# Recurrence prepared within the value projection, head norms in sixteen rows, and more unread products, in a two-block transformer kernel

## The reference

```python
def rwkv_features(h, ...):
    kk = heads(k * k_k)
    kk = kk * lax.rsqrt(jnp.maximum(jnp.sum(kk * kk, axis=-1, keepdims=True), 1e-24))   # norm of each head
    ...
    decay = jnp.exp(-jnp.exp(-jax.nn.softplus(-w_raw) - 0.5))
    a = jax.nn.sigmoid(heads(a0[d] + (xa @ a1[d]) @ a2[d]))

def wkv_scan(...):        # first over the context, then over x, forward and backward
    S = (S * w_t[:, :, None, :]
         - jnp.einsum('bhij,bhj->bhi', S, kk_t)[..., None] * kka_t[:, :, None, :]
         + v_t[..., None] * k_t[:, :, None, :])
    y = jnp.einsum('bhij,bhj->bhi', S, r_t)

def rwkv_readout(y, r, k_sum, v, g, r_k, ln_g, ln_b, wo, dtype):
    mean = jnp.mean(y, axis=-1, keepdims=True)
    var = jnp.mean(jnp.square(y - mean), axis=-1, keepdims=True)
    yn = ((y - mean) * lax.rsqrt(var + GN_EPS)).reshape(B, L, D_MODEL) * ln_g + ln_b
    bonus = (jnp.sum(r * k_sum * r_k, axis=-1, keepdims=True) * v).reshape(B, L, D_MODEL)
    return ((yn + bonus) * g) @ wo

def context_attention(q, k, v):
    p = jax.nn.softmax(q k^T * NA_HEAD_DIM ** -0.5)
    return p v
```

## Time and profile before

| | us |
|---|---|
| median of 3 runs | 2656.08 |
| lowest, highest | 2654.51, 2663.36 |
| profiled execution | 2654.95 |
| its span | 2653.2 |
| granted clock, mean over the span | 0.937 |

### The profile page before, as it was taken

One profiled execution on the slowest core, in us unless ns is written; L12 is line 12 of the kernel. 1 busy time (PEld: TensorE's weight loads), 2 busy tenths in 40 slices (PEclk: granted clock), 3 DMA queues, 4 the chain that ended last, 5 costly groups with the idle time before them and its releaser, 6 DMA issues.

```text
span 2653.2 us, 46388 instructions
## 1 busy us (share of the span) xinstructions
PE 2372.0 (89%) x19956; PEld 1958.6 (74%) x19956; DVE 1750.3 (66%) x3332; ACT 1021.3 (38%) x1892; POOL 67.0 (3%) x70
## 2 busy tenths in 40 slices
PE   6899978999989978889887889997989999997998
PEld 5775457787766567778886789996677879666886
DVE  6966788766745476767766578665355865754577
ACT  2134242322321223543332354344245654543465
POOL 0300000000000000000000000020000011000000
PEclk9897989999999989999999899997779999997999
DMA  7420426556522100000001377730045853002475
GB/s 299 145 109 1 173 100 250 211 209 230 213 113 81 47 0 3 3 3 3 3 11 66 145 269 290 267 144 32 1 159 214 334 191 138 12 1 96 180 296 205
DMA packets 47278, 347.99 MB, mean 131 GB/s; under 512 B 5248, under 2 KB 5248, under 8 KB 5728
## 3 DMA queue, kind: packets, MB, share of 16 engines
q1 hardware_dynamic: 45936, 334.52, 33.7%
q0 software_dynamic: 1136, 10.50, 1.0%
HBM read 343.95 MB, written 1.05 MB: 130 GB/s over the span
## 4 chain that ended last, share of the span: by engine, by line
PE 73%; DVE 20%; ACT 4%; issue 2%; DMA 1%; DVEq 0%; ACTq 0%; POOLq 0%
PE banks L533 23%; PE banks L927 8%; PE banks L1775 5%; DVE arena L612 3%; PE banks L1022 3%; PE banks L2520 3%; PE banks L2521 3%; PE banks L2522 3%; PE banks L1001 3%; PE banks L782 2%; PE banks L1652 2%; PE banks L1846 2%; PE banks L2551 1%; PE banks L2553 1%; PE banks L2552 1%
## 5 line engine op out<-in xcount | busy, mean ns | idle before, releaser
L612 DVE SCALAR_TENSOR_TENSOR arena<-weight_slots,silu_c,arena 128x256 f32<-128x256 f32 x776 | 328.3, 495 | 0.0
L514 DVE TENSOR_TENSOR moe_w_low<-weight_slots,moe_w_high 128x2048 fp32r<-128x2048 f32 x96 | 218.0, 2289 | 71.9 <-ACT moe_w_high L505 71.0
L927 PE MATMUL banks<-arena,weight_slots 128*128 128x256 f32 (+1 forms) x768 | 231.8, 460 | 19.0 <-DVE arena L1567 11.7
L927 PEld LDWEIGHTS banks<-arena,weight_slots 128*128 128x128 f32 x768 | 149.3, 196 | 95.4 <-issue 73.9
L505 ACT ACTIVATE moe_w_high<-weight_slots 128x2048 fp32r<-128x2048 f32 x96 | 181.3, 1911 | 24.7 <-PE banks L2553 19.8
L505 ACT ACTIVATE mlp_w_high<-weight_slots 128x2048 fp32r<-128x2048 f32 x64 | 122.2, 1910 | 170.6 <-PE banks L533 124.6
L1775 PE MATMUL banks<-weight_slots,arena 64*64 64x64 f32 (+1 forms) x3648 | 150.8, 225 | 36.8 <-DVE weight_slots L2088 15.5
L514 DVE TENSOR_TENSOR mlp_w_low<-weight_slots,mlp_w_high 128x2048 fp32r<-128x2048 f32 x64 | 146.3, 2286 | 48.5 <-ACT mlp_w_high L505 48.4
L1775 PEld LDWEIGHTS banks<-weight_slots,arena 64*64 64x64 f32 x3648 | 141.6, 136 | 44.9 <-issue 16.3
L2520 PE MATMUL banks<-moe_w_high,slots_x 128*128 128x512 f32 x320 | 133.5, 417 | 11.8 <-DVE moe_w_low L514 11.8
L1927 ACT ACTIVATE weight_slots<-banks 128x512 f32<-128x512 f32 x80 | 47.8, 597 | 230.1 <-DVE weight_slots L2088 201.7
(11 more groups left out here) (384 smaller groups left out, 5119.9 us busy)
## 6 DMA issues: line engine op xcount, KB each, us to landing
weight_slots<-weights SPq DMA_DIRECT2D x318, 1024.0 KB, 4.8
arena<-small POOLq DMA_DIRECT2D x1, 2560.0 KB, 9.0
arena<-x_t POOLq DMA_DIRECT2D x1, 2048.0 KB, 16.6
arena<-bias POOLq DMA_DIRECT2D x1, 2048.0 KB, 9.5
constants<-consts POOLq DMA_DIRECT2D x1, 1395.0 KB, 21.1
out_t<-arena SPq DMA_DIRECT2D x1, 1024.0 KB, 3.9
parameters<-params POOLq DMA_DIRECT2D x1, 775.0 KB, 9.9
arena<-pool_inv POOLq DMA_DIRECT2D x1, 512.0 KB, 10.4
```

What stands on the lines that cost most here:

```text
L514: nc.vector.tensor_tensor(self.pair(j)[1], slot(j, 0, SLOT), self.pair(j)[0], ALU.subtract).then_inc(*v.step("used", j))
L612: nc.vector.scalar_tensor_tensor(a_, w, c, a_, ALU.mult, ALU.add).then_inc(*v.step())
L927: ins = nc.tensor.matmul(psum(b, 0, w), slot(j, k, 256, i * P, P), moving(k), start=(k == 0), stop=(k == KT - 1))
```

## The change

1. **Head norm of the removal keys.** The eight sums go by accumulation into one tile of 16 rows (a row per head, new constant heads), behind wv block 0. One maximum, root and reciprocal of 16x512 replace eight of each. A constant SPREAD of 16x1024 (a copy) is the stationary operand of eight products that bring the 16 rows back to 128 behind wv block 1; the removal-key instruction reads them from PSUM.
2. **Chunk 0 of the recurrence** is prepared within the value projection. wkv_tensor and wkv_vector get parts: raws(0) behind block 1, orders(0) and raws(1) before the last half block; VectorE's part 0 behind its copies of block 1, part 1 behind those of block 2. ScalarE's sigmoids and decays of chunk 0 stand after its copies of block 1.
3. **Steady chunks.** raws(c+2) stand behind orders(c+1) at a chunk's end, no longer at level 1. raw_in(c+1) follows the masks. running(c+1,0) is at level 1, running(c+1,1) at level 2 ahead of turned, and ScalarE's sigmoids(c+1) stand ahead of inverse_out at level 1.
4. **Readout.** The variance of the eight tiles is accumulated into 16 rows, with one root, one reciprocal of 16x256, and eight spreading products; the bonus products have a loop of their own ahead.
5. **Unread products.** Context, causal and differential attention are filled too, context's into bank 6. The fill is 512 columns wide in the first 8 steps and 256 in the later ones, in sparse attention too (8 wide, 27 narrow).
6. **Router.** One unread product of 512 columns ahead of the counts and three behind them.

The diff, cut to its core:

```diff
-        def fill():
-            nc.tensor.matmul(psum(7), cn("ones"), cn("ident", 0, 512), start=True, stop=True)
+        def fill(u, b):
+            w = 512 if u < RAISE else 256
+            nc.tensor.matmul(psum(b, 0, w), cn("ones"), cn("ident", 0, w), start=True, stop=True)
...
         class ContextAttention(LatentAttention):
             name = "context_attention"
+            filled = True
+            fill_bank = 6
...
-            def kk_sum(t):
-                b = take_bank(pe, ("kk_sum", t))
-                pe.wait_ge(*after("kk_squares", t))
-                nc.tensor.matmul(psum(b), cn("block_ones"), root_of(t), start=True, stop=True).then_inc(*pe.step("kk_sum", t))
+            def kk_sums():
+                b = take_bank(pe, ("kk_sum",), [6])
+                for t in range(KT):
+                    pe.wait_ge(*after("kk_squares", t))
+                    ins = nc.tensor.matmul(psum(b, 0, 512, slice(0, 16)), head_rows(t), root_of(t), start=(t == 0),
+                                           stop=(t == KT - 1))
+                ins.then_inc(*pe.step("kk_sum"))
+
+            def kk_spread(tiles):
+                for t in tiles:
+                    b = take_bank(pe, ("kk_spread", t), range(6))
+                    pe.wait_ge(*after("kk_inverse"))
+                    nc.tensor.matmul(psum(b), head_columns(t), HEAD_ROOT, start=True, stop=True).then_inc(
+                        *pe.step("kk_spread", t))
...
                 for seg in range(2):
-                    b = take_bank(pe, ("wv", jj, seg))
+                    if (jj, seg) == (3, 1):
+                        wkv_tensor(pe, 1)
+                        pe.stage("project_wv")
+                    b = take_bank(pe, ("wv", jj, seg), range(6))
...
                 if jj == 0:
+                    pe.stage("removal_key")
+                    kk_sums()
                     low_rank("g", "g1", 1, [X])
-                    pe.stage("project_wv")
+                elif jj == 1:
+                    pe.stage("removal_key")
+                    kk_spread(range(KT))
+                    wkv_tensor(pe, 0)
...
-            raws(0)
-            for d in range(2):
-                orders("bm", 0, d, WK["B"][:, d], "beta")
-            for d in range(2):
-                orders("gm", 0, d, WK["G"][:, d], "gamma")
+            if part == 0:
+                raws(0)
+                return
+            if part == 1:
+                for d in range(2):
+                    orders("bm", 0, d, WK["B"][:, d], "beta")
+                for d in range(2):
+                    orders("gm", 0, d, WK["G"][:, d], "gamma")
+                raws(1)
+                return
...
                     if lv == 1:
                         seed(c, 0)
                         seed(c, 1)
-                        if c < 7:
-                            raws(c + 1)
...
+                if c < 6:
+                    raws(c + 2)
...
-                    if ahead and lv == 3:
+                    if ahead and lv == 2:
                         running(c + 1, 1)
...
                     if ahead and lv == 1:
-                        raw_in(c + 1)
-                    if ahead and lv == 2:
                         running(c + 1, 0)
...
-                v.wait_ge(*after("taken", "y_var", t))
-                nc.vector.reciprocal(RD[:, t], RD[:, t]).then_inc(*v.step())
-                v.wait_ge(*v.own)
-                stt(YC[:, t], YC[:, t], pr("lng", t, 1), RD[:, t], ALU.mult, ALU.mult).then_inc(*v.step())
+            spread_vector(v)
+            v.wait_ge(*after("taken", "y_var"))
+            nc.vector.reciprocal(RD[0:16, 0], RD[0:16, 0]).then_inc(*v.step("y_inverse"))
+            for t in range(KT):
+                v.wait_ge(*after("y_spread", t))
+                stt(YC[:, t], YC[:, t], pr("lng", t, 1), psum(bank_of(("y_spread", t)), 0, SEQ), ALU.mult, ALU.mult).then_inc(
+                    *v.step("taken", "y_spread", t))
...
         class CausalAttention(Attention):
             name, n, base = "causal_attention", 16, ATT_B
+            filled = True
...
+            unread(1)
             pe.wait_ge(*after("sorting"))
...
+            unread(3)
```

More of the change, by code:

```diff
@@ L1143, in bass_two_blocks @@
             filled = False
+            fill_bank = 7
             subtract = False
@@ L1666, in squares @@
                     nc.scalar.activation(root_of(t), KR[:, t], ACT.Square, scale=pr("kk", t, 1)).then_inc(*act.step("kk_squares", t))
-            def roots(tiles):
-                for t in tiles:
-                    act.wait_ge(*after("taken", "kk_sum", t))
-                    nc.scalar.activation(root_of(t), root_of(t), ACT.Sqrt).then_inc(*act.step("kk_root", t))
             x_squares_scalar(act, "n1_1", "x02", CTX, YT)
@@ L1688, in features_scalar @@
             act.stage("removal_key")
-            squares(range(KT - 1))
-            act.wait_ge(*after("mix", "g", KT - 1))
-            squares([KT - 1])
+            squares(range(KT))
             def after_block(jj):
-                roots(kk_tiles(jj))
                 if jj == 0:
@@ L1928, in inverse_out @@
                     *act.step("inverse_t", c, d, lv))
-            sigmoids(0)
-            load_table(act, ACT.Exp)
-            for d in range(2):
-                decays(0, d)
+            if first:
+                sigmoids(0)
+                load_table(act, ACT.Exp)
+                for d in range(2):
+                    decays(0, d)
+                return
             for c in range(8):
```

150 lines of the change are left out of this document (97 added, 53 removed).

## The result

| | before | after |
|---|---|---|
| median, us | 2655.52 | 2623.23 |
| lowest, highest | 2654.51, 2663.36 | 2621.91, 2623.98 |
| profiled execution | 2654.95 | 2623.69 |
| its span | 2653.2 | 2621.9 |
| granted clock, mean | 0.937 | 0.955 |

The ratio is 0.9867, with a 95% interval from 0.985 to 0.9885: the changed kernel is faster by 32.3 us, in four executions each. Forecast were 2598 and a gain of 57. The time is inside the range of 2580 to 2628 and right in sign, but 25 us of the gain are missing. It lies outside the forecast's own range of 2584 to 2611: the wider range holds it only because it was drawn to take in rivals, and 2623 is within 1 us of the 2624 of a rival that did not happen. That is luck.

A forecast was written before the change was run, and what follows sets the result against it. TensorE was taken as the bound (73% of the chain), either slow at its lower clock or waiting for VectorE; terms summed to −58.3, with +1 for constants and instructions −57.3, giving 2598 us, range 2580 to 2628 (own range 2584 to 2611).

The forecast's parts named there:

- the 2624 of a rival: Even mixer: only differential and causal attention stay at the lower clock, +18 instead of −7.1; two thirds of chance 0.17.
- eight spreads of 0.86: Value projection: eight new spreading products behind wv block 1 add 6.9 us on PE, within a term of −15.5.
- The cover: Value projection: DVE's part 0, 18.5 us, fits beside PE's block 2 and half of block 3, 20.7; if short, −9.
- a chunk's grow starts 1.3 to 1.6 us earlier in six chunks: Steady chunks: gain by the order of time, before about 1.0 is given back; term −3, bounds −9 and +8.
- What is given back by the earlier running: Steady chunks: running(c+1,1) ahead of level-2 transposes makes ScalarE's inverse_out some 2 us later, losing about 1.0 of the 1.6.
- one round through PE: Readout: 0.6 us for the first spread, within +3.3 of new work against −14.0 of reciprocals; term −10.7.
- 34 × 0.075 = −2.5: Projection behind the readout: 34 products start at the higher clock, as PE idles less; 0 if the clock is low.
- Half of 2.81: Context attention: at the upper level a step's own work takes 1.41 us; with fills, the term is −8.5.
- 34.5, against DVE's 28.44 ... I take 38: Even mixer, 1840 to 1884: PE's work with fills is 34.5 us; stretch taken as 38 for 44, −6.
- The rival by which narrow fills don't hold the clock: Sparse attention: 256-column fills from step 8 on lose the clock, +74 and −10.5 lost, 2683 us; chance 0.05.
- The rivals of a filled stage that stays low: Filled stages stay at 1.2 GHz: differential and causal alone give 2624, context attention 2630; chance 0.17.
- Rival (b): The rearranged recurrence does not pay: +4 instead of −3 and −9 instead of −15.5, 2612 us; chance 0.10.

The follow-up runs named there:

- the first of the two combined kernels: Changed kernel with spreading products of 128 rows and, in context attention alone, later unread products 128 columns wide: 2609.18 us (0.9826 of before).

## Why the prediction was right or wrong

**Value projection.** The step that failed is "eight spreads of 0.86". The price was right at the upper level, at which the first of them still run (0.43 for each of the two records of a product), but the clock fell under them: they cost 1.31 each on average and left the lower level to the raws, 5.3 us together. The rest of the sum was right: with 128 rows the term is −15.0, against −15.5. The cover held; VectorE's part 0 ended at 968.3, and orders started at 972.2, the moment PE was through with the first half of block 3.

**Table load.** The trace of after shows ScalarE's next instruction again right behind the load (955.31, for a load of 1.28 us at 954.02). There is no loss by the drain that the Trainium skill (ScalarE: Activation LUTs, What ACT_TABLE_LOAD costs) has; the row was the better guide.

**Steady chunks.** The step that failed is "a chunk's grow starts 1.3 to 1.6 us earlier in six chunks". From grow to grow, chunks 0 to 2 gained 1.0 us each (forecast 0.6), but chunks 3 to 6 lost 1.3, 1.0, 0.6 and 1.0. With running back at level 3, chunks 0 to 2 gain 1.6 each, but the later ones only 0.3 each on average, and the term is −6.1: the gain comes in three chunks. What is given back by the earlier running was right, in mechanism and size: 7.1 us over seven chunks, where 1.0 for each was forecast. Part of the loss in chunks 3 to 6 may be the clock, since the changed kernel is at 0.50 for 3.4 us in each of them and the kernel before in two of the four; this was not separated. Growing chunks were named as a sign of being wrong, and in chunks 3 to 6 it came.

**Readout.** Two steps failed. The loop was priced on VectorE alone, 14 us less of reciprocals; that PE's work in it, 2 × 0.43 a tile, would become the bound at the lower level was not priced, since the new products were taken for "one round through PE". From the mean to the start of the projection it is 4.2 us less, where 10.7 were forecast. And "34 × 0.075 = −2.5" took 34 products as given, while those are what was left after 14 had run in the loop's idle time: without the idle time they stand behind it, and the projection's part is 2.4 us more instead of 2.5 less. With 128 rows both come back: the projection's part is −2.6, and the whole term −12.0 against −13.2.

**Context attention.** Right in kind, −6.7 for −8.5. Half of 2.81 was too little for a step's own work: a filled step takes 2.43 with 512 columns and 2.01 with 256 (start of the values at 240.71, 243.14; 245.15, 247.16 in the trace of after), where 2.37 and 1.94 were forecast. Over 16 steps that is 1.1 of the 1.8 us; the rest was not followed up.

**Even mixer.** The step "34.5, against DVE's 28.44 ... I take 38" was wrong by 3.9 us. The 38 hold the head norms and causal attention, which came out at 1.9 and 39.95 us, where before they were 3.7 and 40.29: of the 4.1 us that causal attention was to give, 0.3 came. It is bound by the turns between PE, VectorE and ScalarE. The busy time of VectorE is no bound by itself where each unit goes to and fro. The head norms (−1.8 for −1.9) and the projection's start (−1.1) were right. Differential gained 0.8 where 0 was taken.

**Sparse attention.** −8.1 for −10.5, for the reason that was named: VectorE and ScalarE end next. The rival by which narrow fills don't hold the clock did not come true at 256 columns in this stage, nor at 128; at 128 it did in the causal part, and at 256 two traces (64 rows; running at level 3) fell there for 6.8 us.

**Routers.** −3.9 for −0.5: 2.9 us between the first gathering product of layer 0 and sparse attention, 0.8 in the second router. Little of this is the unread products': without them the first of these stretches is 314.9 us, with them 314.6, and before it was 317.5. Where the rest comes from stays open.

**Before the change's first place** the profile has 2.5 us more than before, in the attention ahead of context attention, which stays at the lower level to 192 instead of 187. Nothing is changed there, and among the profiles of the experiments some have it (another 181 to 192) and others don't.

The rivals of a filled stage that stays low, and of the slower kernel, were not what happened. Rival (b), the recurrence that doesn't pay, came in part: its −9 for the value projection is near the −9.6 measured, by another cause, and the steady chunks did lose by ScalarE's chain. Most of the miss, 15.5 us of the 25 by the two stretches, came from an edit that was taken to be settled: the new products themselves lowered the clock. The rest are gains taken too large in the steady chunks, the causal part, sparse and context attention, against 3.4 us that the routers' part gave beyond the forecast.

## What to carry to other kernels

Price a new product by the clock it leaves behind as well as by its columns: one that uses few rows of the array costs no less time, and here took the clock from work around it; stationary operands filled up with rows of zeros gave it back and made the kernel 16 us faster. When a VectorE loop is shortened, add up what TensorE has in it and what ran in TensorE's gaps, since both come due. In a chain between three engines an operation moved one place earlier on VectorE can be waited for on ScalarE; one line moved back was worth 7 to 8 us of the recurrence.

## What the runs showed of the hardware

- In the value projection TensorE's clock followed how many rows a product uses: with PE busy throughout, it fell to 0.51 under eight spreads of 16 rows by 512 columns, and with 64 and with 128 rows it stayed at 1.00. Head sums with 128 rows and 16 columns of weights stayed at 1.00 (7.04 us for 8). The duration of a product at one level did not depend on the rows: at the upper level the records of a spread by 512 columns start 0.43 us apart with 16 rows (936.23, 936.65) and with 128 (7.03 us for 16), and at the lower level a spread of 16 rows by 256 columns takes the 1.22 us of a gate product of 128 rows.
- Alternating with products of 128 rows behind a wait of 2.86 us, spreads of 16 and of 64 rows stayed at 0.50 to the end of the loop, and spreads of 128 rows came back to 1.00 within 4 us, or in one trace of the three with them (the first of the two combined kernels) never fell.
- One stretch can run at either level in executions of the same kernel: the compression products and the start of sparse attention ran at 0.50 for 48 us in one execution of 2627.03 us, with PE busy 48.00 of 48, and four others took 2605.39 to 2612.59 at a higher mean clock.
- The clock fell at 939.2 though PE had been busy for 14.00 of 14 us. The Trainium skill (TensorE: Matmul & The Clock Gate, What's actually happening) has the lower level follow idle time; the trace disagrees here.
